# Projections in the order xr, q, xr, q, kv, gates, the first group by pairs of x blocks, q kept by group, and gelu in its accumulator bank

## The reference

```python
h = rmsnorm(x, norm1_g)
q, k, v, xr, gate = split(h @ w_in)        # 512, 128, 128, 512, 512 columns
q, k = rope(rmsnorm(q)), rope(rmsnorm(k))  # 8 q heads, 2 kv heads, 64 wide
attn = softmax(q k^T / 8) v                # per sequence
xc = conv4(xr)                             # depthwise, centred
r, i = sigmoid(blockdiag(xc)), sigmoid(blockdiag(xc))   # for each direction
a = exp(-8 r softplus(-lam)); b = sqrt(1 - a*a) * i * xc
h_lru = scan_forward(a, b) + scan_reverse(a, b)
x = x + concat(attn, h_lru * gelu(gate)) @ w_out
y = x + expert_choice_moe(rmsnorm(x, norm2_g))   # 16 experts, top 64 tokens of each sequence
```

## Time and profile before

| | us |
|---|---|
| median of 3 executions (1078.15 to 1079.59) | 1079.47 |
| the profiled execution | 1081.51 |
| its span, first to last instruction | 1079.7 |
| TensorE, VectorE, ScalarE, POOL busy | 991.9, 813.7, 708.3, 336.0 |
| mean granted clock of TensorE | 0.970 |

### The profile page before, as it was taken

How to read it: one execution, slowest core, us unless ns; L and a number is a source line. 1 busy time by engine, 2 the same in 40 slices (tenths; PEclk the granted TensorE clock), 3 DMA queues, 4 the chain that set the end, 5 groups by cost and what they waited for, 6 DMA issues and landing times.

```text
span 1079.7 us, 14786 instructions
## 1 busy us (share of the span) xinstructions
PE 991.9 (92%) x4935; PEld 824.2 (76%) x4935; DVE 813.7 (75%) x1030; ACT 708.3 (66%) x931; POOL 336.0 (31%) x190
## 2 busy tenths in 40 slices
PE   3999999978899999934999999999999999999995
PEld 3789997866766788833788888888888888888874
DVE  5658789867798322263898889988898889888883
ACT  6367767566798211141898777877797778877773
POOL 0000040065366000041064346533663356413320
PEclk9999999999999999966999999999999999999997
DMA  6111101000301543386899999999999999999851
GB/s 247 51 45 45 44 13 40 1 1 1 117 1 61 197 155 118 117 318 233 312 381 387 386 393 399 383 390 393 390 392 383 386 392 403 385 383 373 310 167 28
DMA packets 75232, 248.95 MB, mean 231 GB/s; under 512 B 9356, under 2 KB 16568, under 8 KB 75192
## 3 DMA queue, kind: packets, MB, share of 16 engines
q1 hardware_dynamic: 70584, 231.64, 56.0%
q0 software_dynamic: 4608, 16.78, 6.2%
HBM read 231.63 MB, written 16.78 MB: 230 GB/s over the span
## 4 chain that ended last, share of the span: by engine, by line
PE 77%; DVE 10%; ACT 7%; issue 3%; DMA 1%; SPq 0%; POOL 0%; ACTq 0%; POOLq 0%
PE bank L934 23%; PE bank L936 23%; PE bank L935 23%; PE bank L940 5%; DVE e_lo L1460 2%; ACT e_hi L865 2%; PE bank L1094 1%; PE bank L1057 1%; PE bank L1058 1%; ACT prob L825 1%; DMA x_nat<-in_x_prompt_dram 1%; DVE probT_lo L1398 1%; DVE row_stat L1386 1%; DVE top_idx L1445 1%; ACT probT_hi L818 1%
## 5 line engine op out<-in xcount | busy, mean ns | idle before, releaser
L934 PE MATMUL bank<-e_hi,xsT_hi 128*128 128x512 f32 x512 | 201.7, 394 | 1.6 <-DVE xsT_lo L1465 1.4
L936 PE MATMUL bank<-e_hi,xsT_lo 128*128 128x512 f32 x512 | 199.8, 390 | 0.0
L935 PE MATMUL bank<-e_lo,xsT_hi 128*128 128x512 f32 x512 | 199.8, 390 | 0.0
L639 POOL COPY idx_now<-idx_all 128x1 uint32 (+1 forms) x16 | 157.0, 9811 | 28.1 <-DMA y_dram<-ys,idx_now 28.1
L865 ACT ACTIVATE e_hi<-raw_gate 128x1024 fp32r<-128x1024 f32 x128 | 134.6, 1060 | 35.3 <-PE bank L936 33.8
L1460 DVE TENSOR_TENSOR e_lo<-raw_down,e_hi 128x1024 fp32r<-128x1024 f32 x128 | 146.9, 1220 | 2.4 <-ACT e_hi L865 0.6
L1460 DVE TENSOR_TENSOR e_lo<-raw_up,e_hi 128x1024 fp32r<-128x1024 f32 x128 | 146.7, 1219 | 1.4 <-ACT e_hi L865 1.3
L1460 DVE TENSOR_TENSOR e_lo<-raw_gate,e_hi 128x1024 fp32r<-128x1024 f32 x122 | 141.2, 1219 | 4.6 <-ACT e_hi L865 4.6
L865 ACT ACTIVATE e_hi<-raw_up 128x1024 fp32r<-128x1024 f32 x128 | 126.4, 1055 | 1.7 <-PE bank L936 0.3
L865 ACT ACTIVATE e_hi<-raw_down 128x1024 fp32r<-128x1024 f32 x128 | 125.2, 1060 | 1.1 <-PE bank L936 0.9
L934 PEld LDWEIGHTS bank<-e_hi,xsT_hi 128*128 128x128 f32 x512 | 96.5, 189 | 22.3 <-DVE xsT_lo L1465 1.8
(11 more groups left out here) (217 smaller groups left out, 2086.4 us busy)
## 6 DMA issues: line engine op xcount, KB each, us to landing
raw_gate<-in_exp_w_gate_dram SPq DMA_DIRECT2D x64, 1024.0 KB, 10.7
raw_up<-in_exp_w_up_dram SPq DMA_DIRECT2D x64, 1024.0 KB, 8.3
raw_down<-in_exp_w_down_dram SPq DMA_DIRECT2D x64, 1024.0 KB, 7.1
w_raw<-in_w_in_dram SPq DMA_DIRECT2D x7, 1024.0 KB, 5.2
wo_raw<-in_w_out_dram SPq DMA_DIRECT2D x8, 512.0 KB, 4.3
y_dram<-x SPq DMA_DIRECT2D x8, 512.0 KB, 5.5
h_rows<-h SPq DMA_DIRECT2D x8, 512.0 KB, 3.3
x_nat<-in_x_prompt_dram SPq DMA_DIRECT2D x4, 512.0 KB, 5.9
```

What stands on the lines that cost most here:

```text
L639: pool.tensor_copy(idx_now[:, 2:3], idx_all[:, bass.ds(e, 1)] if not isinstance(e, int) else idx_all[:, e:e + 1]).then_inc(idx_copied, 1)
L934: pe.matmul(out, l_hi, r_hi, start=first, stop=False)
L935: pe.matmul(out, l_hi, r_lo, start=False, stop=False)
L936: return pe.matmul(out, l_lo, r_hi, start=False, stop=last)
```

## The change

The order of groups becomes xr, q, xr, q, kv, gate, gate. The first group is projected by pairs of x blocks: 8 steps of 24 matmuls of 256 columns, two channel halves for each pair, between the turning of further blocks. Its weights are loaded, and split, in two halves; those of group 1 have a tile of their own. `qkv` becomes `q_nat`, by group, and `kv_nat`, so that q can be prepared once its own group is there: in 10 units of 512 columns (two blocks of one q group, or four blocks of k), each with square, sum, rotate (three full-width instructions; the sine table's signs are swapped to fit) and norm. Units 0 to 3 come at jobs 5 to 8, units 4 to 8 at 14 to 19, the rotation and norm of unit 9 in slots 3 and 4 of the attention. POOL's late steps are gone; POOL now makes `wo_lo` of the first six blocks of w_out in VectorE's place. The recurrence starts two jobs later, `xr_pad` holds two channel tiles, `ib` and `mult` change places from tile to tile, and the scan's two multiplications come ahead of its scans. `w_lo` of a group is made three or four jobs before it is used, behind the scan of that step. The copies of xr out of PSUM go from VectorE to ScalarE. Gelu is written back into its bank, where VectorE reads it; the last four jobs use banks 4 to 7, and the first eight turns wait for the product of their bank. The split of blocks 4 and 5 moves from jobs 26 and 27 into slots 6, 7, 10 and 11. SP loads g1b and two blocks of x, then w of group 0, two more blocks of x, w of group 1, vectors, the rest of x, and the tables.

```diff
-    GROUPS = [("xr", 0, XR0), ("xr", 2, XR0 + GW), ("qkv", 2 * GW, 2 * GW), ("qkv", 0, 0), ("qkv", GW, GW),
+    GROUPS = [("xr", 0, XR0), ("q", 0, 0), ("xr", 2, XR0 + GW), ("q", 1, GW), ("kv", 0, 2 * GW),
               ("gate", 0, GATE0), ("gate", 2, GATE0 + GW)]
+    KV_G = 4
...
-    xr_pad = at("xr_pad", R1 + 104 * K, [P, CT, SEQS, XP], F32)
-    R2 = R1 + 104 * K + 16480
+    xr_pad = at("xr_pad", R1 + 104 * K, [P, 2, SEQS, XP], F32)
...
+    def ib_of(ct, d):
+        return (ib, mult)[ct % 2][d]
+
+    def mult_of(ct, d):
+        return (mult, ib)[ct % 2][d]
...
-    ORDER = [(g, j) for g in range(3) for j in range(JOBS)]
-    ORDER += [(g, j) for half in range(2) for g in (3, 4) for j in (2 * half, 2 * half + 1)]
-    ORDER += [(g, j) for g in (GATE_G, GATE_G + 1) for j in range(JOBS)]
+    SEMS_OF = {"xr": xr_out, "gate": gated, "q": q_out, "kv": kv_out}
+
+    BY_CHANNEL = (0, 2, 1, 3)
+    ORDER = [(g, BY_CHANNEL[j] if GROUPS[g][0] == "xr" and g else j) for g in range(NG) for j in range(JOBS)]
...
+    def job_bank(n):
+
+        return n % 4 if n < NG * JOBS - 4 else 4 + n % 4
...
+    HALF = S // 2
+    steps = [("square_x", 0), ("norm_x", 0), ("square_x", 1), ("norm_x", 1), ("turn_x", 0), ("turn_x", 1),
+             ("w_hi", 0, 0), ("w_lo", 0, 0), ("hi_x", 0), ("lo_x", 0), ("w_hi", 0, 1), ("w_lo", 0, 1)]
+    for b in range(2, NB + 1):
+        if b < NB:
+            steps += [("square_x", b), ("norm_x", b)]
+        steps += [("hi_x", b - 1), ("lo_x", b - 1)]
+        if b < NB:
+            steps.append(("turn_x", b))
+        if b == 3:
+            steps.append(("vectors",))
+        if b == 6:
+            steps += [("w_hi", 1), ("w_lo", 1)]
+        steps.append(("project_pair", b - 2))
+        if b == 6:
+            steps += [("empty", 0), ("empty", 1)]
+    steps += [("project_pair", NB - 1), ("empty", 2), ("conv", 0)]
...
+    LRU_FROM = (5, 9, 13, 17)
...
+    for u, n in enumerate((5, 6, 7, 8)):
+        lru_at(n, ("square", u), ("sum", u), ("rotate", u))
+    lru_at(5, ("softplus",))
+    for ct, c in enumerate(LRU_FROM):
+        lru_at(c + 1, ("gates", ct, 0))
+        lru_at(c + 2, ("gates", ct, 1))
+        lru_at(c + 3, ("decay", ct))
+        if ct < CT - 1:
+            lru_at([8, 12, 16][ct], ("conv", ct + 1))
+        lru_at(c + 4, ("scan", ct))
...
+    for u, n in enumerate((14, 14, 17, 18, 19, 20), 4):
+        lru_at(n, ("square", u), ("sum", u), *([("rotate", u)] if u < UNITS_QK - 1 else []))
+    NORM_ORDER = (0, 1, 4, 5, 8, 2, 3, 6, 7, 9)
+    BATCHES = ((0, JOBS), (JOBS, UNITS_QK))
+    for batch, n in enumerate((13, 21)):
+        lru_at(n, ("rstd", batch))
+    for u, n in zip(NORM_ORDER, (21, 21, 21, 21, 21, 24, 24, 25, 25)):
+        lru_at(n, ("norm", u))
+    for b, n in enumerate((22, 22, 23, 23)):
+        lru_at(n, ("hi", b), ("lo", b))
+    lru_at(26, *[(stage, n) for stage in ("transpose", "out") for n in range(BPS)])
...
-            if n == max(FIRST_OF[w - 1], LAST_OF[w - 2] + 1 if w >= 2 else 0):
+        for w in range(2, NG):
+            if n == FIRST_OF[w] - (0, 0, 3, 3, 3, 3, 4)[w]:
...
-    beside = {2: [("v", 0)], 15: [("hi", 6)], 16: [("lo", 6)], 23: [("hi", 7)], 24: [("lo", 7)]}
-    LATE_STEPS = [("swap", 0), ("swap", 1), ("swap", 2), ("cos", 0), ("cos", 1), ("cos", 2), ("add", 0), ("add", 1), ("scale", 0), ("scale", 1)]
-    for i, b in enumerate(range(EARLY_BLOCKS, NB)):
-        for k, part in enumerate(LATE_STEPS):
-            beside.setdefault(3 + 10 * i + k, []).append(("late", (b, part)))
+    beside = {2: [('v', 0)], 3: [('rotate', 9)], 4: [('norm', 9)], 6: [('hi', 4)], 7: [('lo', 4)], 10: [('hi', 5)], 11: [('lo', 5)], 15: [('hi', 6)], 16: [('lo', 6)], 22: [('hi', 7)], 23: [('lo', 7)]}
...
+        return n if n < BPS else 4 + n % BPS if n < EARLY else 7
...
+        load_x(0)
+        sp.dma_start(g1b[:, :], norm1_g[0:1, :].to_broadcast([P, D])).then_inc(g1_loaded, 16)
+        load_x(1)
+        first = w_in[0, :, GROUPS[0][2]:GROUPS[0][2] + GW].rearrange("(k p) n -> p k n", p=P)
+        for part in range(2):
+            ks = slice(part * KC // 2, (part + 1) * KC // 2)
+            sp.dma_start(w_raw[:, ks, :], first[:, ks, :]).then_inc(w0_loaded[part], 16)
+        for b in range(2, BPS):
+            load_x(b)
+        sp.dma_start(w1_raw[:, :, :], w_in[0, :, GROUPS[1][2]:GROUPS[1][2] + GW].rearrange("(k p) n -> p k n", p=P)).then_inc(w1_loaded, 16)
+        for at_row, rows_in in rows:
+            sp.dma_start(vec_rows[at_row:at_row + rows_in.shape[0], :], rows_in).then_inc(vec_loaded, 16)
+        for b in range(BPS, NB):
+            load_x(b)
+        load_tables()
+        sp.wait_ge(pool_ready, 5)
+        load_bd(0)
...
+            if kind == "split_lo" and n < 2 * WO_EARLY:
+                k, cols = n // 2, slice(n % 2 * D // 2, (n % 2 + 1) * D // 2)
+                pool.wait_ge(wo_hi_done, n + 1)
+                pool.tensor_tensor(wo_lo[k][:, cols], wo_raw[k][:, cols], wo_hi[k][:, cols].bitcast(F32), ALU.subtract).then_inc(wo_lo_pool, 1)
...
-                    n = JOBS * (g - GATE_G) + j
-                    act.wait_ge(scan_done, CT)
-                    if n >= 2:
-                        act.wait_ge(gated, n - 1)
-                    act.wait_ge(proj_done, nth + 1)
-                    act.activation(gate_now[:, n % 2, :], bank[:, nth % 4, :], ACT.Gelu_apprx_tanh).then_inc(gate_out, 1)
...
+                    act.activation(bank[:, job_bank(nth), :], bank[:, job_bank(nth), :], ACT.Gelu_apprx_tanh).then_inc(gate_out, 1)
+                elif what == "xr":
+                    if c0:
+                        act.wait_ge(xc_done, c0 + j % 2 - 1)
+                    act.activation(xr_pad[:, j % 2, j // 2, CONV_LEFT:CONV_LEFT + S], bank[:, job_bank(nth), :], ACT.Copy).then_inc(xr_out, 1)
...
-                    act.wait_ge(scan_done, ct)
-                act.activation(ib[d][:, :], bank[:, 6:8, :].rearrange("p a b -> p (a b)"), ACT.Sigmoid,
+                    act.wait_ge(scaled, 2 * (ct - 1) + d + 1)
...
+            if n < 2 * BPS:
+                pe.wait_ge(gated, n + 1)
...
+            elif kind == "project_pair":
+                t, c = divmod(arg[0], 2)
+                pe.wait_ge(ht_lo_done, BPS * (t + 1))
+                src, tok, ch = slice(2 * t * P, 2 * (t + 1) * P), slice(t % 2 * 2 * P, (t % 2 + 1) * 2 * P), slice(c * P, (c + 1) * P)
+                for k in range(KC):
+                    if t == 0 and c == 0 and k % 4 == 0:
+                        pe.wait_ge(w0_lo_done, k // 4 + 1)
+                    ins = product(bank[:, t // 2 * 2 + c, tok], w_hi[:, 0, k, ch], w_lo[:, 0, k, ch], hT_hi[:, k, src], hT_lo[:, k, src],
+                                  k == 0, k == KC - 1)
+                if t % 2:
+                    ins.then_inc(proj_done, 1)
...
-                if n >= 4:
+                    pe.wait_ge(wlo_done, g)
+                if n >= NG * JOBS - 4:
+                    pe.wait_ge(sigm_done, 4 * CT)
+                else:
                     pe.wait_ge(*evacuated(n - 4))
...
+                dve.tensor_tensor(turned[:, :].rearrange("p (b h d) -> p b h d", b=nb, h=h), heads, sin, ALU.mult).then_inc(turned_done, 1)
+                dve.wait_ge(turned_done, n + 1)
+                dve.tensor_tensor(heads, heads, cos, ALU.mult).then_inc(scaled_cos, 1)
+                dve.wait_ge(scaled_cos, n + 1)
+                quarters = unit(n).rearrange("p (m o d) -> p m o d", o=2, d=HD // 4)
+                dve.tensor_tensor(quarters, quarters, turned[:, :].rearrange("p (m o d) -> p m o d", o=2, d=HD // 4)[:, :, ::-1, :],
+                                  ALU.add).then_inc(rotated, 1)
...
-                    link(dve.tensor_tensor(ib[d][:, :], ib[d][:, :], mult[d][:, :], ALU.mult))
+                    dve.tensor_tensor(ib_of(ct, d)[:, :], ib_of(ct, d)[:, :], mult_of(ct, d)[:, :], ALU.mult).then_inc(scaled, 1)
+                for d in range(2):
+                    dve.wait_ge(scaled, 2 * ct + d + 1)
+                    x = ib_of(ct, d)
```

More of the change, by code:

```diff
@@ L310, in layer_program @@
-    for b in range(BPS):
-        prepare_at(PREP_FROM + 5 + b // 2, ("hi", b), ("lo", b))
-    for b in range(BPS, NB):
-        prepare_at(PREP_FROM + 6 + (b - BPS) // 2, ("square", b), ("sum", b))
-    prepare_at(PREP_FROM + 7, ("rotate", BPS))
-    prepare_at(PREP_FROM + 8, ("rstd", 1), ("rotate", BPS + 1))
-    prepare_at(PREP_FROM + 8, *[(stage, n) for stage in ("transpose", "out") for n in range(BPS)])
-    for b in range(BPS, EARLY_BLOCKS):
-        prepare_at(PREP_FROM + 9, ("norm", b))
@@ L319, in layer_program @@
-    for b in range(BPS, EARLY_BLOCKS):
-        prepare_at(PREP_FROM + 10, ("hi", b), ("lo", b))
+    HALF = S // 2
[14 more added lines that the diff above has]
+            steps += [("empty", 0), ("empty", 1)]
@@ L1223, in prepare @@
[L1223 to L1236 removed]
+                dve.wait_ge(tabs_done, 5)
@@ new lines, in prepare @@
+                dve.wait_ge(*unit_ready(n))
+                if n:
```

(10 more changed lines are left out.)

411 lines of the change are left out of this document (163 added, 248 removed).

## The result

The changed kernel takes 1069.66 us (median of 4 runs, 1067.15 to 1070.87), the kernel before 1079.53 us beside it (4 runs): a ratio of 0.9899, 95% interval 0.9865 to 0.9933. Timed again with the experiments it takes 1070.69 us against 1080.17, ratio 0.9901 [0.9882, 0.9921]. So it is faster by 9.5 to 9.9 us; forecast were 7.3, and 1072.2 us with a range of 1067.0 to 1078.2, which holds both medians.

A forecast was written before the change was run, and what follows sets the result against it. Bounds: TensorE's work, start and one stall in projections; the softmax chain, later VectorE and ScalarE, in attention. Terms -5.9 - 4.0 + 1.5 + 0.4 + 3.2 - 2.5 = -7.3 us gave 1072.2 us, range 1067.0 to 1078.2.

The forecast's parts named there:

- Point 1: Start of projections: the first group, by pairs of x blocks, starts at 18.0 us and ends at 47.8; gain 5.9 us.
- Rival C: Start of projections: the new start brings nothing, as loads or VectorE are no earlier; 1078.1 us, chance 0.10.
- Point 2: Projections at 167.6 us: TensorE's stall for w_lo goes, 2.2 us, and the lower clock behind it, 1.8; gain 4.0.
- Point 3: First recurrence period: w_lo of group 3, behind the scan, comes late and job 12 waits; price 1.5 us.
- Rival B: First recurrence period: VectorE becomes the bound, gates(1, 0) waits too, the clock falls; 7 us instead of 1.5, 1077.7 us, chance 0.15.
- The edits priced at nothing: Copies of xr on ScalarE, POOL's removed steps, split multiplications and ib and mult by turns: each worth nothing.
- Point 5: Early attention: unit 9's rotation and norm and the splits of blocks 4 and 5 burden VectorE; price 3.2 us.
- Point 4: End of projections: gelu written back into its bank makes the fourth turn wait; price 0.4 us.
- lo 7: Early attention: this step leaves the slot in which mixA_lo also stands; gain 1.0 us.
- Rival A: Early attention and the late w_lo: the new work is hidden and costs 0; 1067.5 us, chance 0.15.
- Point 6: Late attention: wo_lo moves from VectorE to POOL, and the stage goes from 42 to 39.5 us; gain 2.5.
- Rival D: Late attention: POOL becomes the bound, the stage takes 49.4 us, 7.4 longer; 1082.1 us, chance 0.09.

The follow-up runs named there:

- e5: Changed kernel with x blocks 2 and 3 loaded ahead of the first group's weights again, as in the kernel before; pairs stay: 1072.25 us, ratio 0.9913.
- e1: Changed kernel with its first group projected again by whole jobs behind four blocks of x, not by pairs; loads and list order stay: 1081.05 us, ratio 0.9997.
- e6: Kernel before the change, with squares, sums and rotations of blocks 2 and 3 one job later, behind w_lo: 1082.13 us, ratio 1.0010.
- e11: Changed kernel with w_hi of group 3 moved on ScalarE behind the sigmoids of gates(1, 0): 1070.65 us, ratio 0.9909.
- e4: Changed kernel with the second sigmoid of a tile waiting again for the whole scan of the tile before: 1074.69 us, ratio 0.9943.
- e10: Changed kernel with rotation and norm of unit 9 moved from attention slots 3 and 4 to job 27, second timing: 1066.54 us, ratio 0.9867.
- e7: Changed kernel with rotation and norm of unit 9 and the hi and lo splits of blocks 4 and 5 moved to job 27: 1066.91 us, ratio 0.9872.
- e8: The changed kernel timed again, nothing altered, beside other runs of its set: 1070.69 us, ratio 0.9901 to the kernel before.
- e2: Changed kernel with the twelve wo_lo of the early w_out blocks moved back from POOL to VectorE: 1074.17 us, ratio 0.9940.

## Why the prediction was nearly right

The time lies inside the likeliest case (1069.5 to 1075), near its lower end. By the two profiled executions the six terms should have been some 4.9 us larger in sum (12.2 where 7.3 stood, up to the output projection); by the medians 2.2 to 2.6. The misses by term below are read in the profiled executions.

**Point 1, the first group: mechanism right, size short.** Predicted -5.9, measured -7.25. The first pair started at 17.48 (predicted 18.0), and the group took 28.97 us (29.8): the terms for waits and for the lower clock were too generous. e5 confirms the part of the loads and e1 that the gain needs the pairs. In the nine executions with this start the gain is 6.3 to 7.5 us (job 4 at 46.2 to 47.3), so it lies about the upper end of 7 that I gave, and in this one above it. Rival C is out.

**Point 2, the stall: -4.0, as predicted**, and its second half, the clock, is confirmed by e6. The wait of 0.3 us for a sigmoid at 153.19 us, which went as well, wasn't in the sum. e6 also shows that moving rotations away from w_lo isn't enough: where they and their squares go has to have room.

**Point 3, what becomes late: +1.5 predicted, 0.8 measured.** The adding-up put xc_lo at 16.0 us, w_lo at 28.9 and job 12 at 27.4 behind the same zero (75.07 us in this trace); read there, w_lo ended at 28.4 and job 12 started at 28.4. The wait stood one step further ahead, on ScalarE, which I hadn't put in the sum (w_hi, a table load and a sigmoid ahead of the one that frees the bank); e11 moves it to w_lo. Later periods have no wait. So the wait that the sum had did not come, and one that it hadn't did; that the term is only 0.7 off is luck. Rival B, VectorE as the bound of that period, did not come: it idled only 0.53 us between 83.7 and 103.4 us, but w_lo was in time by 0.05.

**The edits priced at nothing: two were not.** The end of POOL's late steps is in point 5. Splitting the multiplications and exchanging `ib` and `mult` I held to be worth nothing since TensorE had no gap there before. That was the wrong question. Before, the first scan ended at 93.9 us, the sigmoid behind it ran from 93.97 to 95.09, and gates(1, 1) began at 95.50: 0.4 us of slack. In the new order the scan ends at 101.2 and gates(1, 1) is due at 99.8, and e4 shows over 4 us lost without the edit. The sum came out right although this step of it was wrong, and only because the change contains both the new order and this edit: that is luck.

**Point 4, gelu in its bank:** 0.25 us of wait, predicted 0.4.

**Point 5, early attention: +3.2 predicted, +1.8 measured** from slot 2 on (1.6 from slot 0). All traces have the same marks in this stage, and the times from one to the next show the parts. From slot 5 to the first turn that waits for kT: 13.11 us before, 16.80 in the changed kernel, 14.37 with unit 9 moved (e10), 13.11 with the splits of blocks 4 and 5 moved too (e7). So rotation and norm of unit 9 cost 2.4 (predicted 2.8), the splits 1.3 (1.4). Against their 3.7 stand 1.9, where I had 1.0 for lo 7, and the record shows other causes for them. The first stands ahead of the next turn that waits for kT:

```profile
251.43 1.16 POOL L591 TENSOR_TENSOR qkv<-qkv,tab 128x256 f32<-128x256 f32 x1
251.93 0.94 DVE L1243 TENSOR_TENSOR k_pair<-qkv,k_pair 128x256 fp32r<-128x256 f32 x1
253.61 1.09 PE L940 MATMUL bank<-ident,q_pair 128*128 128x128 f32 x4 [2.00 <-DVE kT L1252]
```

```profile
244.91 0.41 DVE L1255 TENSOR_TENSOR k_pair<-kv_nat,k_pair 128x256 fp32r<-128x256 f32 x1
246.07 0.63 PE L944 MATMUL bank<-ident,q_pair 128*128 128x128 f32 x4 [1.46 <-DVE kT L1264]
```

The first three lines are of the kernel before, the others of the changed one. A subtraction of VectorE took 0.94 us beside a late step of POOL, and takes 0.41 without one. From the first of these turns to the second TensorE takes 13.16 us in both traces with POOL's late steps (before, e6) and 12.62 or 12.63 in all eleven without (the changed kernel and its variants). So the end of those steps, which I priced at nothing, was worth 0.5, as the traces read; no run changes it alone. The second cause is the clock. From the second turn to the third TensorE takes 12.11 us before and 10.73 now, since a stretch at the lower clock fell there before and not now. With none there it is 10.7 in five traces, with one 12.0 to 12.2 in seven (the kernel before is one of them), and 13.44 in e8, where it is twice as long. So 1.4 of the 1.9 is chance: two executions of the changed kernel differ by 2.7 us here. Nothing is seen of lo 7's 1.0: the two stretches behind, to the wait for mixA_lo and to the next turn, take 6.99 and 7.61 us before, 7.06 and 7.61 now. With the clock as before the term would have been the predicted 3.2: it would have come out by luck, 0.4 too much for unit 9, 0.1 for the splits, and 0.5 of POOL's steps in place of 1.0 of lo 7. Rival A, these costs hidden, is out.

**Point 6, late attention: -2.5 predicted, -3.3 measured**, and e2 gives it to this edit alone. By that the stage of 42 us went to 38.7, nearer to the 38.0 of POOL's sum at its short durations than the 39.5 that I took. POOL's subtractions are 1.28 to 1.30 us in all 18 cases, and its idle time for reciprocals fell from 14.0 to 3.5 us. Rival D needed POOL's sum to pass 47 us and half of that idle time to stay: the sum is 17.2 + 14.2 + 9.0 = 40.4. It is close to being the bound all the same, with three waits of TensorE for prob (0.74, 0.31 and 0.47 us); so is ScalarE, busy for 39.3 of 42 us. The Trainium skill's rule against elementwise work on GpSimd (GPSIMD Engine Reference, Engine selection) would have left this gain: its cost per instruction is there (1.29 us against 0.77 in the mean on VectorE), but the engine had the time. The Trainium skill's Key points on the same page name the contention with VectorE; the trace shows it ending, as forecast, and e2 shows it again.
